# Output product of a hybrid decoder layer: seven half-size products in place of eight

## The chip, the cores and the metric

The kernel runs on one core of one Trainium2 chip. Its metric is the device time of one execution in microseconds (us), taken in three runs. TensorE (PE) multiplies matrices from SBUF into the eight banks of PSUM, VectorE (DVE) and ScalarE (ACT) read PSUM and SBUF, GpSimd (POOL) works from SBUF to SBUF, and SyncE (SP) issues DMAs.

## The reference, cut to what matters

```python
merged = sigmoid(g_a) * (y_a @ w_branch_a) + sigmoid(g_b) * (y_b @ w_branch_b)
x = x + gate[:, None, :] * (merged @ w_out)
```

`y_a` comes from a pooling branch, `y_b` from a sparse attention with top-k keys. All matrices are float32; `merged` is 1024 tokens by 1024 channels, `w_out` 1024 by 1024. This case is about the last line and the sum before it.

## The kernel before, in words

Every exact product is made of three passes: each operand is split into a high part (a copy rounded to the type fp32r) and a low part (what is left), and `product` (L727) adds high x high, high x low and low x high into one PSUM bank (L729 to L731). ACT makes the high parts, POOL or DVE the low ones by a subtraction.

The last part of the program goes as follows; times are of the profiled execution.

- Branch b (until 724): 16 units, each one bank of 128 channels by 512 tokens from 12 matmuls (`branch_b`, L1119). For each, DVE multiplies the bank by the stored sigmoid and adds branch a's share, read back from DRAM (`merge`, L2234, two tiles of `e_in`). This gives `m_raw`, the transposed `merged`, in four slots. ACT writes its high part `mT_hi`; the low part is made by POOL for even units (L1849) and by DVE for odd ones (`merge_low`, L2245). The order of units is the table `UNITS_B` (L158).
- The weights come in chunks of 256 columns and 1024 rows (four rows of 128 to a piece, `split_piece_hi` and `split_piece_lo`, L664 to L672), two chunks at a time. POOL splits w_branch_b's last two pieces and the first chunk of `w_out` beside the units; DVE splits the low parts of the other three (L1917, through `split_chunk_v`).
- Output product (724 to 813): `WO_ORDER` (L147) gives 20 units: 12 of 128 tokens by 512 columns (24 matmuls of 512) and 8 of 256 columns (24 of 256). Two banks alternate. DVE multiplies each by `gate` (L2304) and adds the rows of x (L2307), ACT issues the store (L1629), and SP loads the next rows.

Each engine runs its own list in order, with waits on semaphores; nothing reorders it. The order is written out by hand, and pools of PSUM banks are named by the table `pp_uses` with `pp_bank`: a use waits until the bank's previous use has been read.

Three smaller places are touched: the wait before the `ga` units (L1077), POOL's last `causal_scores` (L1719), and ACT's first use of SiLU in the attention part.

## Time and profile before

| | us |
|---|---|
| median of 3 runs (lowest to highest) | 816.81 (814.96 to 818.93) |
| profiled execution, its own time | 818.22 |
| its span, first to last instruction | 816.5 |
| busy: PE, DVE, ACT, POOL | 799.7, 579.0, 351.9, 336.7 |

The span is what the trace shows; the execution's own time is 1.7 us more. A matmul's row shows a duration that overlaps with the next one's, so the pace of PE is read from start to start. Starts of DVE instructions overlap their predecessors by less than 0.1 us. The mean granted clock of PE was 0.993 of full speed.

### The profile page before, as it was taken

To read this page: it belongs to the slowest core of one execution; us is meant where nothing else is said; L and a number is where in the kernel's file an instruction comes from. 1 tells how busy PE (TensorE), PEld (TensorE's weight loads), DVE (VectorE), ACT (ScalarE), POOL (GpSimd) and SP (SyncE) were. 2 spreads that over 40 slices of the span, in tenths; PEclk is the share of its full clock that TensorE was granted. 3 is DMA by queue.
4 is the path that set the end of the run, shared out by engine and by line. 5 is a ranking of instruction groups with operands and counts; after the bars stand their busy time and mean duration, and the time that the engine had idled before them with its cause. 6 is when DMAs were issued, how large, how long until landed. Compare 5 with 4: busy or idle time off the path is not lost.

```text
span 816.5 us, 12769 instructions
## 1 busy us (share of the span) xinstructions
PE 799.7 (98%) x4419; PEld 680.0 (83%) x4419; DVE 579.0 (71%) x1198; ACT 351.9 (43%) x644; POOL 336.7 (41%) x311
## 2 busy tenths in 40 slices
PE   7999999999999999999999999999999999999998
PEld 5988998887888888888878877789888897888987
DVE  5877478797888888898898716456667885772522
ACT  5665456664222212223241222687778883420100
POOL 1100524153445468852662212575888812540000
PEclk9899999999999999999999999999999999999999
DMA  9940110013242220331123323743433113753431
GB/s 342 386 126 1 53 52 27 1 41 121 103 123 78 91 90 16 102 96 46 52 78 103 104 78 107 236 138 114 130 105 115 40 40 137 252 168 123 131 101 58
DMA packets 59880, 87.87 MB, mean 108 GB/s; under 512 B 5513, under 2 KB 36525, under 8 KB 59822
## 3 DMA queue, kind: packets, MB, share of 16 engines
...
## 4 chain that ended last, share of the span: by engine, by line
PE 86%; DVE 6%; ACT 3%; issue 2%; DMA 1%; DVEq 1%; SPq 0%; POOLq 0%; POOL 0%; ACTq 0%
PE pp L729 21%; PE pp L730 21%; PE pp L731 21%; PE pp L1182 4%; PE pt L1157 3%; PE ps L970 3%; PE ps L969 3%; DVE score L2110 2%; DMA scale_w<-in_w_ada 1%; DVE prob L2268 1%; PE pt L1090 1%; DVE pT L2198 1%; PE ps L1067 1%; DVE ada_acc L1911 1%; PE pp L875 1%
## 5 line engine op out<-in xcount | busy, mean ns | idle before, releaser
L2135 DVE TENSOR_SCALAR_CACHE_REDUCE junk<-score,cand 128x384 uint8<-128x384 f32 (+1 forms) x186 | 168.6, 944 | 19.3 <-issue 13.3
L729 PE MATMUL pp<-hT_hi,w_hi 128*128 128x512 f32 x384 | 150.0, 390 | 0.8 <-ACT mixed L1511 0.8
L731 PE MATMUL pp<-hT_hi,w_lo 128*128 128x512 f32 x384 | 149.5, 389 | 0.0
L730 PE MATMUL pp<-hT_lo,w_hi 128*128 128x512 f32 x384 | 149.4, 389 | 0.0
L672 POOL TENSOR_TENSOR w_lo<-w_raw,w_hi 128x1024 fp32r<-128x1024 f32 x39 | 96.2, 2484 | 117.0 <-ACT w_hi L667 115.7
L729 PEld LDWEIGHTS pp<-hT_hi,w_hi 128*128 128x128 f32 x384 | 72.1, 188 | 16.1 <-ACT mixed L1511 1.3
L731 PEld LDWEIGHTS pp<-hT_hi,w_lo 128*128 128x128 f32 x384 | 72.1, 188 | 15.2
L730 PEld LDWEIGHTS pp<-hT_lo,w_hi 128*128 128x128 f32 x384 | 72.1, 188 | 14.7
L2198 DVE TENSOR_TENSOR pT<-pt,pT 128x512 fp32r<-128x512 f32 (+3 forms) x96 | 50.6, 555 | 45.0 <-ACT pT L1585 42.0
L1469 ACT ACTIVATE stage<-pp 128x512 f32<-128x512 f32 x32 | 19.2, 599 | 127.3 <-PE pp L731 127.3
L667 ACT ACTIVATE w_hi<-w_raw 128x1024 fp32r<-128x1024 f32 x52 | 52.8, 1054 | 44.8 <-PE pp L731 40.9
L729 PE MATMUL pp<-w_hi,hT_hi 128*128 128x256 f32 (+1 forms) x208 | 69.0, 332 | 1.8 <-POOL w_lo L672 1.1
L730 PE MATMUL pp<-w_lo,hT_hi 128*128 128x256 f32 (+1 forms) x208 | 67.5, 324 | 0.0
L731 PE MATMUL pp<-w_hi,hT_lo 128*128 128x256 f32 (+1 forms) x208 | 67.4, 324 | 0.0
L729 PE MATMUL pp<-w_hi,mT_hi 128*128 128x512 f32 (+1 forms) x160 | 55.6, 348 | 0.2 <-DVE o_row L2304 0.2
L730 PE MATMUL pp<-w_lo,mT_hi 128*128 128x512 f32 (+1 forms) x160 | 55.5, 347 | 0.0
L731 PE MATMUL pp<-w_hi,mT_lo 128*128 128x512 f32 (+1 forms) x160 | 55.5, 347 | 0.0
L729 PE MATMUL pp<-yT_hi,w_hi 128*128 128x512 f32 x128 | 52.7, 411 | 0.8 <-ACT a_out L1533 0.8
L1593 ACT ACTIVATE prob<-prob,neg_max 128x128 f32<-128x128 f32 (+7 forms) x64 | 49.8, 779 | 3.3 <-DVE neg_max L2268 3.0
L2110 DVE SCALAR_TENSOR_TENSOR score<-rel,w_idx,score 128x384 f32<-128x384 f32 (+5 forms) x42 | 43.7, 1042 | 9.3 <-ACT rel L1430 6.1
L2304 DVE TENSOR_TENSOR o_row<-pp,gate 128x512 f32<-128x512 f32 (+1 forms) x20 | 11.7, 584 | 54.3 <-PE pp L731 54.3
L730 PE MATMUL pp<-yT_lo,w_hi 128*128 128x512 f32 x128 | 50.1, 391 | 0.0
(311 smaller groups left out, 1834.2 us busy)
## 6 DMA issues: line engine op xcount, KB each, us to landing
w_raw<-in_w_in SPq DMA_DIRECT2D x36, 512.0 KB, 3.7
sgb_spill<-stage ACTq DMA_DIRECT2D x16, 256.0 KB, 2.0
sga_spill<-stage ACTq DMA_DIRECT2D x16, 256.0 KB, 2.0
stage<-sga_spill SPq DMA_DIRECT2D x16, 256.0 KB, 3.4
ma_spill<-stage POOLq DMA_DIRECT2D x16, 256.0 KB, 2.8
gate_w<-in_w_ada SPq DMA_DIRECT2D x16, 256.0 KB, 2.7
w_raw<-in_w_out SPq DMA_DIRECT2D x8, 512.0 KB, 4.7
e_in<-sgb_spill SPq DMA_DIRECT2D x16, 256.0 KB, 3.0
```

What stands on the lines that cost most here:

```text
L667: nc.scalar.activation(hi, raw, ACT.Copy).then_inc(w_hi_done, 1)
L672: nc.gpsimd.tensor_tensor(lo, raw, hi.bitcast(F32), ALU.subtract).then_inc(w_lo_done, 1)
L729: nc.tensor.matmul(o, a_hi, b_hi, start=first, stop=False)
L730: nc.tensor.matmul(o, a_hi, b_lo, start=False, stop=False)
L731: return nc.tensor.matmul(o, a_lo, b_hi, start=False, stop=last)
L969: nc.tensor.matmul(o[:, a:z], q, kt_[:, 0, a:z], start=True, stop=False)
L970: last = nc.tensor.matmul(o[:, a:z], q, kt_[:, 1, a:z], start=False, stop=True)
L1182: last = nc.tensor.matmul(pp[0][:, 0:2 * P], v2[:, t, :], pT[:, u % 2, t, s, :, :].rearrange("p h q -> p (h q)"), start=(t == 0 and s == 0 ...
L1593: nc.scalar.activation(prob[j % 4][:, 0:keys(b)], prob[j % 4][:, 0:keys(b)], ACT.Exp, scale=-1.0, bias=neg_max[:, j % 4:j % 4 + 1], accum_ ...
L2110: ins = v.scalar_tensor_tensor(s, rel[:, n % 2, 0:keys(b)], w, s, ALU.mult, ALU.add)
L2135: v.tensor_scalar(junk[:, n % 2, 0:keys(b)], score[:, score_at(b):score_at(b + 1)], least, None, ALU.is_ge, ALU.add, accum_out=cnt[:, n:n ...
L2198: v.tensor_tensor(pT[:, j // 2 % 2, t0:t1, 1, j % 2, :], pt[n % 2][:, 0:(t1 - t0) * P].rearrange("p (t q) -> p t q", q=P), pT[:, j // 2 % ...
```

## The change

The output product C = A W, with A the merged tokens by channels and W `w_out`, is cut into halves in tokens, channels and columns. Each quarter A11, A12, A21, A22 is 512 by 512, and so is each quarter of W. Seven products of quarters or of sums of them give C, where eight were made before:

S3 = A11 - A21, S1 = A21 + A22, S2 = S1 - A11, S4 = A12 - S2. The products, in order: A11 W11; S3 (W22 - W12); S2 (W22 - W12 + W11); A22 (W22 - W12 + W11 - W21); A12 W21; S1 (W12 - W11); S4 W22.

- `UNITS_B` is put in another order, so that units 0 to 3 are A11, 4 to 7 A21, and then A22 and A12 by turns of two. DVE makes S3, S1, S2, S4 from the merged units (`part_sums`) and the sums of the weights (`wo_sums`), with 16 loads of a piece of 512 KB instead of 8.
- High parts are ACT's. Low parts: POOL makes A11, A22, S1, A12 and the weights of products 1, 4, 5, 6, 7; DVE makes S3, S2, S4 and the weights of products 2 and 3.
- From unit 4 of branch b on, PSUM banks go in turn over six (the two of `ps` count as four halves).
- ACT copies the first two products into SBUF (`u1`, `u3`), DVE adds the others there (`u2`, `u3`), and rows of 512 columns are then multiplied by the gate and x is added, for four of the 16 by POOL.
- The wait before the `ga` units moves to the first tie transpose, one `causal_scores` moves behind a weight split, and a SiLU on one column is added to ACT ahead of a bank copy.

```diff
     UNITS_B = [(i, m, f) for f in range(2) for i in range(2) for m in range(2)]
-    UNITS_B += [(i, m, f) for i in range(2, 4) for f in range(2) for m in range(2)]
+    UNITS_B += [(i, m, f) for i in range(2, 4) for f in (1, 0) for m in range(2)]
+
+    M_PART = {(0, 0): "A11", (0, 1): "A21", (1, 0): "A12", (1, 1): "A22"}
+    UNIT_AT = {(M_PART[i // 2, f], 2 * (i % 2) + m): n for n, (i, m, f) in enumerate(UNITS_B)}
+    PART_OF = {n: part for part, n in UNIT_AT.items()}
...
+    PRODUCTS = ["A11", "S3", "S2", "A22", "A12", "S1", "S4"]
+    UPPER = [1, 0, 1, 0, 1, 0, 1]
+    STAGE_RAW = [0, 2, 2, 2, 0, 2, 0]
+    STAGE_BY_V = (1, 2)
+    W_LOADS = [(0, 0, 0), (0, 0, 1), (1, 1, 2), (1, 1, 3), (0, 1, 0), (0, 1, 1), (0, 0, 0), (0, 0, 1),
+               (1, 0, 0), (1, 0, 1), (0, 1, 2), (0, 1, 3), (0, 0, 0), (0, 0, 1), (1, 1, 0), (1, 1, 1)]
...
+    SUM_LOADS = [(2, 4), (6,), (8,), (10, 12)]
+    STAGE_SUM = {1: 0, 2: 1, 3: 2, 5: 3}
+    ROWS = 4
+    ROWS_BY_P = range(2 * ROWS, 3 * ROWS)
...
-    pp_bank += [(n + 1) % 2 for n in range(len(pp_uses) - len(pp_bank))]
+    pp_uses += [("wo", i, t) for i in range(len(PRODUCTS)) for t in range(4)]
+    pp_bank += [(n + 1) % 2 if n < 4 else [4, 5, 6, 7, 1, 0][(n - 4) % 6] for n in range(len(pp_uses) - len(pp_bank))]
...
+        pp += [ps[n // 2][:, n % 2 * HALF:(n % 2 + 1) * HALF] for n in range(4)]
...
+        WO_SLOT = [w_raw[:, (len(pieces) + n) % RAW] for n in (0, 1, 2)]
+        WO_RAW = [WO_SLOT[0], w_last[:], WO_SLOT[1], WO_SLOT[2]]
...
+                if u == min(MASK_UNIT):
+                    wait_done(pe, pp_done[pp_at[("mix", 1, 3)]], pp_free_a, pp_free_v)
...
-            wait_done(pe, pp_done[pp_at[("mix", 1, 3)]], pp_free_a, pp_free_v)
...
                     pe.wait_ge(w_lo_done, pieces_through[ci])
+                if k == 0 and n == 4:
+                    wait_done(pe, ps_done[-1], ps_free_a, ps_free_v)
+                    wait_done(pe, ps_done[-2], ps_free_a, ps_free_v)
...
+            for i, name in enumerate(PRODUCTS):
+                a_hi, a_lo = parts[name]
+                pe.wait_ge(wo_hi, 2 * i + 2)
+                wo_lo_wait(pe, i)
+                if name in ("S2", "S3", "S4"):
+                    part = (name, 3 if name == "S3" else 1)
+                    pe.wait_ge(part_lo_v, lo_v_at[part])
+                else:
+                    part = (name, 3)
+                    pe.wait_ge(part_lo_p, lo_p_at[part])
+                pe.wait_ge(part_hi, hi_at[part])
+                for t in range(4):
+                    o = pp_claim(("wo", i, t))
+                    tok = slice(t * P, (t + 1) * P)
+                    for k in range(4):
+                        kw = 4 * UPPER[i] + k
+                        last = product(o[:], a_hi[:, k, tok], a_lo[:, k, tok], w_hi[:, :, kw, :], w_lo[:, :, kw, :],
+                                       k == 0, k == 3)
+                    last.then_inc(pp_full, 1)
...
+                    if n == NSEL * H - 1:
+                        nc.scalar.activation(ssx[:, 0:1], ssx[:, 0:1], ACT.Silu)
...
+            def wo_high(st):
+                for a in range(2):
+                    hi, _, raw = wo_home(st, a)
+                    if st in STAGE_SUM:
+                        act.wait_ge(wo_sum, 2 * STAGE_SUM[st] + a + 1)
+                    else:
+                        j = STAGE_LOAD[st] + a
+                        act.wait_ge(wo_in[W_LOADS[j][2]], w_loaded[j])
+                    nc.scalar.activation(hi, raw, ACT.Copy).then_inc(wo_hi, 1)
...
+                if name == "A21":
+                    act.wait_ge(s3_done, k + 1)
+                    part_high("S3", k, gate_acc[:, k % 2 * HALF:(k % 2 + 1) * HALF])
+                    if k == 3:
+                        act.wait_ge(pp_full, chunk_done(name_of[("ga", 3)]))
+                        wo_high(0)
+                    continue
...
+                part_high(name, k, raw_m(n))
+                if name == "A22":
+                    act.wait_ge(s1_done, k + 1)
+                    part_high("S1", k, raw_21[:, k, :])
...
+            wo_high(1)
+            act.wait_ge(s2_done, 4)
+            for p in range(2):
+                pair_high("S2", p, raw_11)
+            keep(0, u1)
+            wo_high(2)
+            keep(1, u3)
+            act.wait_ge(s4_done, 4)
+            for p in range(2):
+                pair_high("S4", p, raw_21)
+            wo_high(3)
+            product_done(act, 2)
+            wo_high(4)
+            for n in range(4):
+                store(n)
+            product_done(act, 3)
+            wo_high(5)
+            for n in range(4, 8):
+                store(n)
+            product_done(act, 4)
+            wo_high(6)
+            for n in range(8, 16):
+                store(n)
...
-            causal_scores(NT - 1)
             pool.wait_ge(w_lo_done, pieces_through[name_of[("zb", 1)]] - 1)
             split_piece_lo(pool, pieces_through[name_of[("zb", 1)]] - 1)
+            causal_scores(NT - 1)
...
+            def part_low(name, k, raw):
+                hi, lo = parts[name]
+                pool.wait_ge(part_hi, hi_at[name, k])
+                gp.tensor_tensor(lo[:, k, :], raw, hi[:, k, :].bitcast(F32), ALU.subtract).then_inc(part_lo_p, 1)
+
...
+                if name == "A21":
+                    if k == 3:
+                        wo_low(0)
+                    continue
+                part_low(name, k, raw_m(n))
+                if name == "A22":
+                    part_low("S1", k, raw_21[:, k, :])
+            wo_low(3)
+            wo_low(4)
+            wo_low(5)
+            wo_low(6)
+            for n in ROWS_BY_P:
+                pool.wait_ge(c22_done, n - ROWS_BY_P[0] + 1)
+                pool.wait_ge(x_row_in[n % 4], 16 * (n // 4 + 1))
+                gp.tensor_tensor(o_row[:, n % 4, :], o_row[:, n % 4, :], x_row[:, n % 4, :], ALU.add).then_inc(o_row_p, 1)
...
+                if n >= 11:
+                    dve.wait_ge(part_hi, hi_at[PART_OF[n - 3]])
+                    dve.wait_ge(part_lo_p, lo_p_at[PART_OF[n - 3]])
...
+                v.tensor_tensor(raw_m(n), pp[pp_bank[u]][:], e_in[:, 0, n % 4, :], ALU.mult).then_inc(pp_free_v, 1)
+                dve.drain()
+                v.tensor_tensor(raw_m(n), raw_m(n), e_in[:, 1, n % 4, :], ALU.add).then_inc(m_raw_done, 1)
...
+            def part_sums(n):
+
+                name, k = PART_OF[n]
+                if name == "A11":
+                    return
+                dve.drain()
+                if name == "A21":
+                    if k == 0:
+                        dve.wait_ge(pt_full, pt_at[("gate", 1)] + 1)
+                    v.tensor_tensor(gate_acc[:, k % 2 * HALF:(k % 2 + 1) * HALF], raw_11[:, k, :], raw_21[:, k, :],
+                                    ALU.subtract).then_inc(s3_done, 1)
+                    if k:
+                        s3_low(k - 1)
+                elif name == "A22":
+                    if k == 0:
+                        s3_low(3)
+                    v.tensor_tensor(raw_21[:, k, :], raw_21[:, k, :], raw_m(n), ALU.add).then_inc(s1_done, 1)
+                    dve.drain()
+                    dve.wait_ge(part_hi, hi_at["A11", k])
+                    dve.wait_ge(part_lo_p, lo_p_at["A11", k])
+                    v.tensor_tensor(raw_11[:, k, :], raw_21[:, k, :], raw_11[:, k, :], ALU.subtract).then_inc(s2_done, 1)
+                else:
+                    dve.wait_ge(part_hi, hi_at["S1", k])
+                    dve.wait_ge(part_lo_p, lo_p_at["S1", k])
+                    v.tensor_tensor(raw_21[:, k, :], raw_m(n), raw_11[:, k, :], ALU.subtract).then_inc(s4_done, 1)
...
+                v.tensor_tensor(WO_RAW[2 + a], WO_RAW[2 + a], WO_RAW[a], op).then_inc(wo_sum, 1)
...
             for n in range(len(MERGE_AFTER), 16):
                 merge(n)
-                if n % 2 == 0:
-                    merge_low(n - 1)
-            merge_low(15)
-            split_chunk_v(name_of[("wo", 1)])
-
-            for n, (i, t) in enumerate(WO_ORDER):
+                part_sums(n)
+                if n >= 14:
+                    wo_sums(0, n - 14, ALU.subtract)
+            dve.drain()
+            wo_low(1)
+            for p in range(2):
+                pair_low("S2", p, raw_11)
+            for a in range(2):
+                wo_sums(1, a, ALU.add)
+            dve.drain()
+            wo_low(2)
+            for a in range(2):
+                wo_sums(2, a, ALU.subtract)
+
...
+            def finish_row(n):
+                o, c0 = o_row[:, n % 4, :], HALF * (n // 8)
+                dve.drain()
+                mult = v.tensor_tensor(o, o, gate[:, c0:c0 + HALF], ALU.mult)
+                if n in ROWS_BY_P:
+                    mult.then_inc(c22_done, 1)
+                    return
+                dve.drain()
+                dve.wait_ge(x_row_in[n % 4], 16 * (n // 4 + 1))
+                v.tensor_tensor(o, o, x_row[:, n % 4, :], ALU.add).then_inc(o_row_done, 1)
+            for t in range(4):
+                dve.wait_ge(pp_free_a, pp_done[pp_at[("wo", 1, t)]][0])
+                o = bank(2, t)
+                v.tensor_tensor(u2[:, t, :], o, u1[:, t, :], ALU.add).then_inc(pp_free_v, 1)
+                dve.drain()
+                v.tensor_tensor(u3[:, t, :], u2[:, t, :], u3[:, t, :], ALU.add)
+            for p in range(2):
+                pair_low("S4", p, raw_21)
+            dve.wait_ge(pt_free_a, pt_done[pt_at[("gate", 1)]][0])
+            dve.drain()
+            for t in range(4):
+                o, row = bank(3, t), take_row(t)
+                v.tensor_tensor(row, u3[:, t, :], o, ALU.subtract).then_inc(pp_free_v, 1)
+                finish_row(t)
+            for a in range(2):
+                wo_sums(3, a, ALU.subtract)
+            for t in range(4):
+                o, row = bank(4, t), take_row(4 + t)
+                v.tensor_tensor(row, o, u1[:, t, :], ALU.add).then_inc(pp_free_v, 1)
+                finish_row(4 + t)
```

The first place where instructions move is DVE's row at branch b's unit 8, of before:

```order
L2242 TENSOR_TENSOR m_raw<-pp0,e_in 128x512
L2244 TENSOR_TENSOR m_raw<-m_raw,e_in 128x512
L2242 TENSOR_TENSOR m_raw<-pp1,e_in 128x512
L2244 TENSOR_TENSOR m_raw<-m_raw,e_in 128x512
L2249 TENSOR_TENSOR mT_lo<-m_raw,mT_hi 128x512
```

Two units take five instructions there. Now, units 8 and 9 (both of A22) and the first of A12 on the same engine, where raw_x is the merged unit, raw_11 and raw_21 hold A11 and A21 and then the sums:

```order
L2428 TENSOR_TENSOR raw_x<-pp1,e_in 128x512
L2430 TENSOR_TENSOR raw_x<-raw_x,e_in 128x512
L2435 TENSOR_TENSOR S3_lo<-gate_acc,S3_hi 128x512
L2454 TENSOR_TENSOR raw_21<-raw_21,raw_x 128x512
L2458 TENSOR_TENSOR raw_11<-raw_21,raw_11 128x512
L2428 TENSOR_TENSOR raw_x<-pp0,e_in 128x512
L2430 TENSOR_TENSOR raw_x<-raw_x,e_in 128x512
L2454 TENSOR_TENSOR raw_21<-raw_21,raw_x 128x512
L2458 TENSOR_TENSOR raw_11<-raw_21,raw_11 128x512
L2428 TENSOR_TENSOR raw_x<-ps0,e_in 128x512
L2430 TENSOR_TENSOR raw_x<-raw_x,e_in 128x512
L2462 TENSOR_TENSOR raw_21<-raw_x,raw_11 128x512
```

A unit of A22 has four instructions and one of A12 three; the low parts of A22, S1 and A12 went to POOL. POOL's last rows of before:

```order
L1849 TENSOR_TENSOR mT_lo<-m_raw,mT_hi 128x512 x3
L672 TENSOR_TENSOR w_lo<-w_raw,w_hi 128x1024
L1849 TENSOR_TENSOR mT_lo<-m_raw,mT_hi 128x512
L672 TENSOR_TENSOR w_lo<-w_raw,w_hi 128x1024
L1849 TENSOR_TENSOR mT_lo<-m_raw,mT_hi 128x512 x2
L672 TENSOR_TENSOR w_lo<-w_raw,w_hi 128x1024 x2
L1849 TENSOR_TENSOR mT_lo<-m_raw,mT_hi 128x512 x2
```

And now, from the same instant (the start of branch b's merges) to the middle of the A22 and A12 units:

```order
L2008 TENSOR_TENSOR A11_lo<-raw_11,A11_hi 128x512 x4
L779 TENSOR_TENSOR w_lo<-w_raw,w_hi 128x1024 x2
L2014 TENSOR_TENSOR w_lo<-w_raw,w_hi 128x1024
L2014 TENSOR_TENSOR w_lo<-w_last,w_hi 128x1024
L2008 TENSOR_TENSOR A22_lo<-raw_x,A22_hi 128x512
L2008 TENSOR_TENSOR S1_lo<-raw_21,S1_hi 128x512
L2008 TENSOR_TENSOR A22_lo<-raw_x,A22_hi 128x512
L2008 TENSOR_TENSOR S1_lo<-raw_21,S1_hi 128x512
L2008 TENSOR_TENSOR A12_lo<-raw_x,A12_hi 128x512 x2
```

Eight parts of 512 became sixteen (eight are shown up to the last row's two of A12, the other six follow in the same pattern), and the four of 1024 stay four, two of them now for the first product.

## Rows read from the trace of the kernel before

**Rows 1.** The page: busy us of each engine, share of span, instructions.
```profile
PE 799.7 (98%) x4419; PEld 680.0 (83%) x4419; DVE 579.0 (71%) x1198; ACT 351.9 (43%) x644; POOL 336.7 (41%) x311
```

**Rows 2.** Windows: length, busy of PE, PEld, DVE, ACT, POOL, clock, DMA, GB/s.
```profile
690.00:724.00 34.00, 34.00 (x151) 27.86 (x149) 27.69 (x34) 13.25 (x19) 21.28 (x11) 1.00 0.68 220
724.00:814.00 90.00, 89.01 (x481) 77.20 (x480) 32.62 (x50) 6.73 (x8) 1.29 (x1) 1.00 0.34 110
```

**Rows 3.** Timeline of VectorE in the output product; start us, us.
```profile
785.73 0.69 DVE L2304 TENSOR_TENSOR o_row<-pp,gate 128x512 f32<-128x512 f32 x1 [3.96 <-PE pp L731]
...
791.17 0.69 DVE L2304 TENSOR_TENSOR o_row<-pp,gate 128x512 f32<-128x512 f32 x1 [3.96 <-PE pp L731]
...
813.24 0.42 DVE L2304 TENSOR_TENSOR o_row<-pp,gate 128x256 f32<-128x256 f32 x1 [1.93 <-PE pp L731]
```

**Rows 4.** Timeline of TensorE, first output units of 256 columns.
```profile
724.39 0.28 PE L730 MATMUL pp<-w_lo,mT_hi 128*128 128x256 f32 x1
...
729.67 0.28 PE L729 MATMUL pp<-w_hi,mT_hi 128*128 128x256 f32 x1
```

**Rows 5.** Tile m_raw and line L672: ns min/median/max, first and last start.
```profile
L2242 DVE TENSOR_TENSOR m_raw<-pp,e_in x16: 677/692/693, 683.2 to 724.2; 128x512 f32<-128x512 f32 x16
L2244 DVE TENSOR_TENSOR m_raw<-m_raw,e_in x16: 692/892/1169, 684.0 to 725.0; 128x512 f32<-128x512 f32 x16
...
L1849 POOL TENSOR_TENSOR mT_lo<-m_raw,mT_hi x8: 1293/1306/1747, 691.0 to 724.2; 128x512 fp32r<-128x512 f32 x8
L2249 DVE TENSOR_TENSOR mT_lo<-m_raw,mT_hi x8: 678/685/2883, 691.4 to 726.8; 128x512 fp32r<-128x512 f32 x8
...
L672 POOL TENSOR_TENSOR w_lo<-w_raw,w_hi x39: 2381/2407/3165, 101.8 to 717.0; 128x1024 fp32r<-128x1024 f32 x39
```

**Rows 6.** Timeline of VectorE from 711 to 728.
```profile
711.38 0.69 DVE L2244 TENSOR_TENSOR m_raw<-m_raw,e_in 128x512 f32<-128x512 f32 x1
711.99 0.69 DVE L2249 TENSOR_TENSOR mT_lo<-m_raw,mT_hi 128x512 fp32r<-128x512 f32 x1
...
716.82 0.79 DVE L2244 TENSOR_TENSOR m_raw<-m_raw,e_in 128x512 f32<-128x512 f32 x1
717.53 2.88 DVE L2249 TENSOR_TENSOR mT_lo<-m_raw,mT_hi 128x512 fp32r<-128x512 f32 x1
720.34 0.68 DVE L2242 TENSOR_TENSOR m_raw<-pp,e_in 128x512 f32<-128x512 f32 x1
721.11 1.01 DVE L2244 TENSOR_TENSOR m_raw<-m_raw,e_in 128x512 f32<-128x512 f32 x1
...
727.40 2.48 DVE L1917 TENSOR_TENSOR w_lo<-w_raw,w_hi 128x1024 fp32r<-128x1024 f32 x2
```

**Rows 7.** Timeline of GpSimd from 714 to 722.
```profile
714.46 5.41 POOL L672 TENSOR_TENSOR w_lo<-w_raw,w_hi 128x1024 fp32r<-128x1024 f32 x2 [0.35 <-ACT w_hi L667]
719.83 1.74 POOL L1849 TENSOR_TENSOR mT_lo<-m_raw,mT_hi 128x512 fp32r<-128x512 f32 x1
```

**Rows 8.** Waits of TensorE: total us, times, longest.
```profile
PE pp L729 <- ACT mixed L1511: 0.8, 1, 0.8
```

**Rows 9.** The page's DMA issues: KB each, median us to landing.
```profile
w_raw<-in_w_out SPq DMA_DIRECT2D x8, 512.0 KB, 4.7
...
out<-o_row ACTq DMA_DIRECT2D x12, 256.0 KB, 3.0
```

**Rows 10.** Last bisection step, first tie transpose, and a table load.
```profile
462.14 0.16 DVE L2151 TENSOR_TENSOR thr<-thr,accept 128x6 int32<-128x6 int32 x1
...
L1055 PE MATMUL pt<-ident_b,eq x33: 219/219/230, 476.3 to 510.9; 128*128 128x128 bf16 x33
...
188.16 1.28 ACT L1395 ACT_TABLE_LOAD   x1
```

**Rows 11.** TensorE's gaps from 185 to 195, in brackets.
```profile
189.89 0.38 PE L729 MATMUL pp<-w_hi,hT_hi 128*128 128x256 f32 x1 [0.45 <-ACT zb_out L1395]
...
194.12 0.50 PE L729 MATMUL pp<-w_hi,hT_hi 128*128 128x512 f32 x1 [1.09 <-POOL w_lo L672]
```

289 lines of the change are left out of this document (178 added, 111 removed).

## The prediction

> **What bounds the kernel now.** I read the page first, then the stretches, then single rows. TensorE (PE) is busy 98% of the span [rows 1]. The output product runs from 724.2 to 813.2, and in both stretches of the tail PE is busy without a break at a granted clock of 1.00 [rows 2]. One 512-column unit of 24 matmuls takes 791.17 - 785.73 = 5.44 us, so 0.227 us a matmul, and a 256-column one costs 0.12 (44 starts from 724.39 to 729.67) [rows 3, 4]. So work taken from PE there is worth its full price, if nothing else is late instead.
>
> What could be late is the second thing to see. While branch b is projected (690 to 724), VectorE (DVE) is busy 27.7 of 34 us and GpSimd (POOL) 21.3 [rows 2], and they are not independent. A DVE add or low part, with both inputs in SBUF, has a shortest time of 0.68 to 0.69 us, but 0.892 in the middle and 2.883 at the longest; the multiply of the same size that reads PSUM stays within 0.677 to 0.693 [rows 5]. The instants say why [rows 6, 7]. POOL's two weight splits last from 714.46 to 719.87. DVE's low part issued at 717.53, inside the second, ends at 720.41, which is 0.54 behind POOL's end. POOL's next, issued at 719.83, lasts 1.74 instead of 1.30 and ends at 721.57, 1.16 behind that DVE end. DVE's add, issued at 721.11, ends at 722.12, 0.55 behind that. They take turns, whole instructions at a time.
>
> A page of the Trainium skill has a rule for it. "SBUF — State Buffer", section "SBUF: two separate sides", says that DVE and GpSimd share a port pair which one instruction holds to its end, and that a DVE instruction takes it when both inputs are in SBUF. The trace agrees (2.883 against 0.68). If both engines ran at once, as their separate queues suggest, the sum below would end near rival A; by the rule it is the forecast. The steps themselves need only the rows.
>
> **The change: what PE gains.** Before, PE runs 12 x 24 matmuls at 0.227 and 8 x 24 at 0.12: 65.3 + 23.0 = 88.3 us. After, 7 products x 4 units x 12 = 336 matmuls of 512 columns: 76.2 us. It gains 12.1, and up to 0.7 of small gaps (813.2 less 724.2 less 88.3). Started at 724.2 and never late, PE would end at 800.4. Six banks in turn take away no wait of branch b, where PE is busy 34.00 of 34.00 us [rows 2].
>
> **What DVE and POOL get.** I count what needs the turn, from 691.0 (POOL's first low part) to where the second product, S3, can start. S3's weight parts come from DVE, and stand behind all merges, part sums and the first weight sum.
> - DVE, 512 wide: 14 adds (units 2 to 15), 4 S3 sums, 4 S3 low parts, 4 each of S1, S2, S4 = 34. Alone one takes 0.61 from start to start (711.38 to 711.99 [rows 6]): 20.7 us.
> - DVE, 1024 wide: two weight sums, two low parts, at 2.48 / 2 = 1.24 [rows 6]: 5.0 us.
> - POOL, 512 wide: 16 low parts (A11, A22, S1, A12), between 1.16 (waiting) and 1.30 (alone); 1.2: 19.2 us. Before there were 8.
> - POOL, 1024 wide: two pieces of w_branch_b and the two of the first product, between 2.26 (waiting: 719.87 less 717.61, the end of DVE's add) and 2.41 (alone) [rows 5 to 7]; 2.35: 9.4 us.
>
> Together 54.3 us, from 691.0 to 745.3. The same count for the kernel before (14 adds, 8 low parts, 8 and 4 on POOL) gives 32.4 of the 36.5 us to 727.5, the end of its last low part, so there it is nearly full already, though PE never waits. POOL's share can't be put off: from unit 11 DVE's multiply waits for the low part of the unit three before (three raw buffers), and each S4 sum for POOL's S1 low part. And the turn is idle where DVE multiplies, 0.77 us (720.34 to 721.11), and POOL has no backlog; writing the instructions down one by one with these durations I find about 3.2 us of it, mostly at units 5 to 7. S3 starts at 748.6. Without lateness it would start at 724.2 + 10.9 = 735.1. **PE waits 13.5 us here**; bounds 9.2 (735.1 to 744.3, no idle turn and the last A12 low part later) and 17 (0.69, 1.30 and 2.41 throughout: 34 x 0.08 + 16 x 0.1 more, less what fills idle turns).
>
> **Products 2 to 4** are ready: behind S3's start DVE needs two S2 low parts, two sums and two low parts (6 x 1.24 = 7.4) within 10.9. The loads, 4.7 us each [rows 9], are asked for as each sum ends. Nothing late.
>
> **S1, the sixth.** Its weight sum stands on DVE behind four rows of the fourth product, each two times 0.69 with some 0.1 of drain and once 0.69, 2.3 us (three operations where before there were two). By the same writing down S3 ends 759.5, S2 770.4, A22 781.2, A12 792.1. DVE first has S4's low parts, which take turns with POOL's splits for A12 to about 777.6, then the four rows (779 to 787.5), the sums to 789.7, then POOL two splits with DVE's work between: 794.9. **2.8 late**; bounds 0 and 4.5.
>
> **S4, the last.** ScalarE (ACT) issues the stores of rows 4 to 7 before it makes the last high part, and row 7 is done near 801.9. One high part of about 1 us later POOL's 2 x 2.4 with DVE between gives 809.1, where PE would be ready at 805.9. **3.2 late**; bounds 0 and 5.
>
> **The end.** Before, 3.3 us from the last matmul (813.2) to the end of the span, with two DVE operations of 0.42 in it [rows 3]. After, three operations of 512 columns (2.3), the store's issue and 3.0 to land [rows 9]: 5.8 us, at most 6.3. **2.5 to 3 more.**
>
> **The middle.** The wait for the last mix banks moves from the start of the ga units to unit 11; PE waited 0.8 for it [rows 8]. What follows is PE's until 476.3, when the tie transposes start, and DVE's bisection ended at 462.3 [rows 10], so it stays gained: -0.8 (bounds -1 and 0). The early SiLU table load (1.28 [rows 10]) now comes in front of a bank copy that PE needs, at 186, and takes away a wait of 0.45 at 189.9 [rows 11]; both run into the 1.09 us wait for POOL's split at 194.1, which follows a DVE split not moved. So 0 (bounds -0.5 and +1). causal_scores moving behind a split of 2.4 us [rows 5] has 13 us of slack before 476.3. 0.
>
> **Sum.** 724.2 + 76.2 + 13.5 + 2.8 + 3.2 = 819.9 for PE's end; + 5.8 = 825.7; - 0.8 = 824.9 for the span, 8.4 over 816.5. The profiled execution took 818.22 for its span of 816.5, the median of the runs is 816.81: 1.41 less. So 818.22 + 8.4 = 826.6 on its own scale, and 825.2 on the median's. I say 825.3.
>
> **Rivals.** (A) DVE and POOL do not get in each other's way in the new order: DVE then needs from 694.4 (unit 4's end) 12 multiplies of 0.77, 32 x 0.61, drains of some 0.15 and 5.0, so until about 731, in time for 735.1; S1 and S4 are in time too. 800.4 + 5.8 - 0.8 = 805.4, the median 805.7: 11 faster. For it speaks that PE never waited on the merges before; against it rows 5 to 7. (B) Turns are taken, but only S3 at its lower bound of 9.2 is late: 800.4 + 9.2 + 5.8 - 0.8 = 814.6, median 814.9, within 0.5% of before. For it speaks that S1 and S4 are each late by some 3 us only, at the end of a chain of DVE, ACT and POOL work of more than 20; against it, that the lower bound leaves the turn never idle. (C) The turn and the forecast's mechanism, with prices at their upper bounds, 17 + 4.5 + 5 and 6.3: 800.4 + 26.5 + 6.3 - 0.8 = 832.4, median 832.7, a slower case of the same sign. (D) Weight loads are late: 16 instead of 8 through four slots. At 4.7 us each and asked for more than 8 us ahead, save the second of W11 and of W21 (5 us ahead), it costs under 2.
>
> **Chances.** 0.70 for the forecast with C, 0.14 for B and what lies near it, 0.16 for A. The point from which it is slower: the gains 12.1, 0.7 and 0.8 less 2.5 at the end are 11.1 us, so the three latenesses together must pass 11.1; by S3 alone, where it starts behind 746. Within 0.5% (4.1 us) is about what a measurement of this kernel can't tell from no change. Faster by more 0.17, within 0.13, slower 0.70. The range is 813 to 832; A alone, and a little above, lies outside. The likeliest case's own range is 819 to 832.
>
> **What the profile will show.** If right: PE idle some 13 us behind A11's product, at about 736, released by DVE's weight low part; smaller gaps of about 3 us before the sixth and seventh products, released by POOL; DVE's two-SBUF-input adds stretched to a median above 1.1 us between 691 and 745, POOL over 75% busy there, multiplies still 0.69; PE matmuls 0.227 apart. Wrong if S3 starts by 738, if the adds stay at 0.7 to 0.9, or if a wait of PE falls on a bank or a load.

## The result

The changed kernel takes 827.88 us (median of 6 runs, 826.28 to 833.5), the kernel before 817.55 (814.82 to 819.21) on the same chips: ratio 1.0152, 95% interval 1.013 to 1.0174. That is slower by 12.4 us by the ratio (one of the waits below is as long by chance). The forecast was slower, at 825.3; the mechanism is the one forecast, with one term missing and three of another size.

The profiled execution took 827.83 us for a span of 826.1. Its page, and TensorE's waits from 690 on (line, what released it, total us, times, longest):

```profile
PE 790.4 (96%) x4275; PEld 667.2 (81%) x4275; DVE 636.5 (77%) x1236; ACT 368.8 (45%) x667; POOL 375.0 (45%) x331
```

```profile
PE pp L836 <- DVE w_lo L2474: 12.4, 1, 12.4
PE ps L836 <- issue: 4.5, 2, 3.2
PE ps L836 <- DVE raw_x L2428: 0.8, 1, 0.8
```

TensorE has 9 us less to do than in [rows 1] and stands for 17.7 us in places where it did not stand before. The stretches of the tail (columns as in [rows 2], which they answer):

```profile
690.00:724.00 34.00, 33.88 (x150) 27.75 (x149) 31.27 (x29) 9.92 (x14) 22.30 (x12) 1.00 0.50 158
724.00:745.00 21.00, 8.42 (x36) 6.30 (x34) 19.55 (x20) 7.33 (x11) 9.77 (x7) 0.83 0.37 121
745.00:830.00 85.00, 70.40 (x288) 57.02 (x288) 65.48 (x69) 17.35 (x22) 26.82 (x12) 0.91 0.46 152
```

PE works 8.4 of the 21 us from 724 while DVE is busy for 19.6, and the granted clock, 1.00 throughout in [rows 2], is 0.83 and 0.91.

**A ruler.** The first stage varies from execution to execution, also where two kernels are the same there: the selection's last wait on ScalarE ends between 178.1 and 182.2 in the 14 profiles taken. So I compare two stretches that don't contain it. The *middle* goes from the end of that wait to the last transposes of the branch stage, the *tail* from there to the end of the span. The four instants, of before and of after:

```profile
181.29 0.50 PE L969 MATMUL ps<-kiT,qiT 128*128 128x512 f32 x1 [0.68 <-ACT rel L1430]
...
688.12 0.60 PE L758 MATMUL pt<-ident,y_row 128*128 128x128 f32 x4
```

```profile
178.13 0.50 PE L1076 MATMUL ps<-kiT,qiT 128*128 128x512 f32 x1 [0.68 <-ACT rel L1540]
...
684.83 0.60 PE L865 MATMUL pt<-ident,y_row 128*128 128x128 f32 x4
```

Before: 506.8 and 816.5 - 688.12 = 128.4. After: 506.7 and 826.1 - 684.83 = **141.3, 12.9 more**. Instants of the tail after stand 3.29 earlier than the same ones on before's scale. Kernels that do the same in the tail differ there by no more than 0.2 us (before and e9_mix_alone 128.4 each, after 141.3 and e7_no_silu 141.5), so a tail, though it comes from one profile, tells smaller differences than the ratios do.

**The turns.** (A turn is the time of one instruction with two SBUF operands, during which such an instruction of the other engine doesn't get on.) GpSimd and VectorE at the A22 units and in the output stage (start us, us):

```profile
708.14 2.55 POOL L2014 TENSOR_TENSOR w_lo<-w_raw,w_hi 128x1024 fp32r<-128x1024 f32 x1 [2.24 <-ACT w_hi L1739]
710.65 2.85 POOL L2014 TENSOR_TENSOR w_lo<-w_last,w_hi 128x1024 fp32r<-128x1024 f32 x1
...
718.20 1.30 POOL L2008 TENSOR_TENSOR A_lo<-raw_x,A_hi 128x512 fp32r<-128x512 f32 x1 [1.30 <-ACT A_hi L1725]
719.46 1.74 POOL L2008 TENSOR_TENSOR S_lo<-raw,S_hi 128x512 fp32r<-128x512 f32 x1
```

```profile
708.53 2.71 DVE L2435 TENSOR_TENSOR S_lo<-gate_acc,S_hi 128x512 fp32r<-128x512 f32 x1
711.16 2.88 DVE L2454 TENSOR_TENSOR raw<-raw,raw_x 128x512 f32<-128x512 f32 x1
...
718.40 1.65 DVE L2458 TENSOR_TENSOR raw<-raw 128x512 f32<-128x512 f32 x1 [0.16 <-issue]
719.97 0.68 DVE L2428 TENSOR_TENSOR raw_x<-ps,e_in 128x512 f32<-128x512 f32 x1
720.74 1.01 DVE L2430 TENSOR_TENSOR raw_x<-raw_x,e_in 128x512 f32<-128x512 f32 x1
```

Each of the first two DVE rows ends 0.54 to 0.55 behind the POOL row it was issued in (711.24 behind 710.69, 714.04 behind 713.50). The fourth, of 719.97, reads PSUM and keeps its 0.68 beside a running POOL instruction.

**The clock.** PE behind its long wait, and the windows around it:

```profile
745.56 0.77 PE L836 MATMUL pp<-w_hi,S_hi 128*128 128x512 f32 x1 [12.38 <-DVE w_lo L2474]
746.13 0.63 PE L837 MATMUL pp<-w_lo,S_hi 128*128 128x512 f32 x1
746.55 0.63 PE L838 MATMUL pp<-w_hi,S_lo 128*128 128x512 f32 x1
...
751.58 0.40 PE L838 MATMUL pp<-w_hi,S_lo 128*128 128x512 f32 x1
751.81 0.39 PE L836 MATMUL pp<-w_hi,S_hi 128*128 128x512 f32 x1
...
795.31 0.47 PE L836 MATMUL ps<-w_hi,S_hi 128*128 128x512 f32 x1 [3.21 <-issue]
...
809.33 0.47 PE L836 MATMUL ps<-w_hi,S_hi 128*128 128x512 f32 x1 [1.29 <-issue]
```

```profile
747.00:749.00 2.00, 2.00 (x6) 1.61 (x5) 2.00 (x3) 1.04 (x3) 0.00 (x0) 0.50 0.00 0
...
752.00:757.00 5.00, 5.00 (x23) 4.13 (x22) 2.91 (x3) 0.83 (x2) 0.00 (x0) 1.00 0.90 305
```

The granted clock is 0.50, the lower level, behind the wait, and matmuls start 0.42 to 0.43 apart (746.13, 746.55) until 751.3, then 0.23. The products from S3 to A12 take 795.31 - 3.21 - 745.56 = 46.5 us, against 4 x 10.9 = 43.6: 2.9 for the clock. S1, behind its 3.2 us wait, takes 809.33 - 1.29 - 795.31 = 12.7 for 10.9: 1.8.

### The profile page after: what moved, and what is told of

Read it like the earlier page. It is cut to its first block, busy times and chain, and to the rows that moved or that the text cites. A ratio compares the mean times of both kernels' runs of the same rounds, so it can differ in the third digit from the quotient of the medians.

```text
span 826.1 us, 12619 instructions
## 1 busy us (share of the span) xinstructions
PE 790.4 (96%) x4275; PEld 667.2 (81%) x4275; DVE 636.5 (77%) x1236; ACT 368.8 (45%) x667; POOL 375.0 (45%) x331
## 4 chain that ended last, share of the span: by engine, by line
PE 77%; DVE 10%; DVEq 6%; issue 3%; ACT 3%; POOL 1%; DMA 0%; POOLq 0%; ACTq 0%
PE pp L836 17%; PE pp L838 17%; PE pp L837 16%; PE pp L1294 3%; PE pt L1269 3%; PE ps L1077 3%; PE ps L1076 3%; DVEq L2429 3%; DVE score L2293 2%; DVEq L2540 1%; DVE o_row L2541 1%; DVE raw_x L2430 1%; PE pp L872 1%; PE pt L895 1%; PE ps L837 1%
## 5 line engine op out<-in xcount | busy, mean ns | idle before, releaser
L779 POOL TENSOR_TENSOR w_lo<-w_raw,w_hi 128x1024 fp32r<-128x1024 f32 x37 | 90.4, 2460 | 129.9 <-ACT w_hi L774 121.0
L2492 DVE CUSTOM_DVE_ANT_0 prob<-ps,bias 128x128 f32<-128x128 f32 (+7 forms) x64 | 47.9, 748 | 3.0 <-PE ps L1077 1.5
L1697 ACT ACTIVATE pT<-pt 128x512 fp32r<-128x512 f32 (+3 forms) x96 | 43.9, 492 | 11.9 <-PE pt L1269 10.9
L774 ACT ACTIVATE w_hi<-w_raw 128x1024 fp32r<-128x1024 f32 x44 | 44.7, 1052 | 4.0 <-ACT stage L1581 2.7
L1269 PE MATMUL pt<-ident,prob 128*128 128x128 f32 x288 | 44.4, 277 | 1.8 <-ACT qT L1664 1.1
L1540 ACT ACTIVATE rel<-ps 128x384 f32<-128x384 f32 (+5 forms) x48 | 36.3, 759 | 19.2 <-PE ps L1077 11.2
L836 PEld LDWEIGHTS pp<-w_hi,hT_hi 128*128 128x128 f32 x208 | 40.2, 193 | 4.2 <-ACT q_all L1477 2.0
L838 PEld LDWEIGHTS pp<-w_hi,hT_lo 128*128 128x128 f32 x208 | 40.2, 193 | 3.3
```

Source lines behind the costliest of these rows:

```text
L774: nc.scalar.activation(hi, raw, ACT.Copy).then_inc(w_hi_done, 1)
L779: nc.gpsimd.tensor_tensor(lo, raw, hi.bitcast(F32), ALU.subtract).then_inc(w_lo_done, 1)
L836: nc.tensor.matmul(o, a_hi, b_hi, start=first, stop=False)
L838: return nc.tensor.matmul(o, a_lo, b_hi, start=False, stop=last)
L1269: last = nc.tensor.transpose(o[:, (t % 4) * P:(t % 4 + 1) * P], prob[j % 4][:, t * P:(t + 1) * P], ident[:])
L1697: nc.scalar.activation(pT[:, j // 2 % 2, t0:t1, 0, j % 2, :], o[:, 0:(t1 - t0) * P].rearrange("p (t q) -> p t q", q=P), ACT.Copy).then_inc ...
```

## The experiments

Theory T: DVE and POOL take turns wherever both read two SBUF operands, and the added sums and low parts make that queue longer than TensorE's work; behind its waits TensorE then also runs at the lower clock. Rival R1: DVE's own list is too long, whatever POOL does. Rival R2: a load, or a chain of dependent steps, is late. A *part* is below a quarter of A or a sum of two (low parts of 512 columns), a *split* the low part of a weight piece (1024 columns), and a *fill* writes zeros and reads nothing. What each kernel took (ratios against the kernel before, run on the same chips):

| kernel | median us | ratio, 95% interval | tail us |
|---|---|---|---|
| before | 816.0 to 817.6 | 1 | 128.4 |
| after | 827.88 | 1.0152 (1.013 to 1.0174) | 141.3 |
| e1_fill | 819.59 | 1.0043 (1.0028 to 1.0059) | 132.3 |
| e2_twice | 830.97 | 1.0170 (1.0147 to 1.0194) | 143.3 |
| e3_s1_vector | 831.05 | 1.0172 (1.015 to 1.0193) | 141.7 |
| e4_early | 822.84 | 1.0065 (1.0044 to 1.0085) | 134.9 |
| e5_warm | 826.73 | 1.0122 (1.0103 to 1.014) | 139.4 |
| e6_late | 828.75 | 1.0153 (1.0122 to 1.0183) | 140.4 |
| e7_no_silu | 828.76 | 1.0158 (1.0134 to 1.0181) | 141.5 |
| e8_best | 822.58 | 1.0080 (1.0057 to 1.0103) | 134.7 |
| e9_mix_alone | 815.18 | 0.9987 (0.9972 to 1.0001) | 128.4 |
| e10_fill_all | 806.69 | 0.9867 (0.9841 to 0.9894) | 118.1 |
| e11_fill_early | 806.04 | 0.9854 (0.9827 to 0.9882) | 117.0 |
| e12_weights_on_vector | 816.84 | 1.0004 (0.9989 to 1.0019) | 129.5 |

**Take POOL's turns away: e1_fill, e10_fill_all.**

```diff
-                gp.tensor_tensor(lo[:, k, :], raw, hi[:, k, :].bitcast(F32), ALU.subtract).then_inc(part_lo_p, 1)
+                gp.memset(lo[:, k, :].bitcast(F32), 0.0).then_inc(part_lo_p, 1)
```

> The changed kernel, with GpSimd's low parts of A11, A22, S1 and A12 (16 subtractions that read two SBUF operands, 1.2 us each in the tally) written as fills with zeros, which read nothing; the low parts of these are left out of the product. Waits, order and signals stay. Theory T (VectorE and GpSimd take turns, a whole instruction each, where both read two SBUF operands): the 19.2 us of these subtractions leave the sequence in which VectorE stands, so the wait of 12.4 us before S3's product falls to 0 to 2 us, the matmuls behind it stay 0.227 us apart instead of 0.427 (2.8 us), VectorE's eight additions to raw_x fall from a mean of 0.93 us towards 0.61 to 0.7, and the kernel comes to about 813 us (809 to 818), about 15 us less than the changed kernel. Rival R1 (VectorE's own list of work up to S3 is too long, whatever GpSimd does): wait and durations as they were, 827 to 828. Rival R2 (a load or the activations' products come late): the same, 827 to 828, with the wait put down to a transfer or to ScalarE.

The tail is 9.0 us shorter. The merged units' additions and multiplies of after, then of this kernel (ns min/median/max):

```profile
L2430 DVE TENSOR_TENSOR raw_x<-raw_x,e_in x8: 693/996/1042, 707.7 to 739.2; 128x512 f32<-128x512 f32 x8
...
L2428 DVE TENSOR_TENSOR raw_x<-ps,e_in x4: 675/680/685, 720.0 to 729.4; 128x512 f32<-128x512 f32 x4
```

```profile
L2430 DVE TENSOR_TENSOR raw_x<-raw_x,e_in x8: 691/692/693, 706.8 to 731.6; 128x512 f32<-128x512 f32 x8
...
736.80 0.76 PE L836 MATMUL pp<-w_hi,S_hi 128*128 128x512 f32 x1 [5.10 <-issue]
```

No edit touched DVE, and its additions fell from 996 to 692 ns; the multiply from PSUM had nothing to lose. The size was missed: I expected the wait to be 0 to 2 us and it is 5.1, and the kernel takes 819.6 and not some 813. Of the 12.4 us, 7.3 are POOL's turns for parts; the next run divides the 5.1.

e10 does the same to POOL's ten splits of output weights (`gp.tensor_tensor(lo, raw, ...)` in `wo_low` becomes `gp.memset(lo, 0)`), and leaves those low parts out too.

> e1_fill with GpSimd's low parts of the output weights (10 subtractions of 1024 columns) written as zero fills too; those low parts are left out. Theory T: VectorE's stretched instructions in the output stage (2.89, 2.11, 2.88, 4.55 for two, 2.35, 2.67, 1.52, 1.48, 1.66 us in the profile after) fall to 0.69 (2.35 for the two of 1024 columns), the low parts are ready 3 us sooner, and the waits before S1's and S4's products (4.5 us together) and their half clock (1 us) go: e1's 819.6 less 5.5 less up to 1 at the end, 813 us (811 to 815.5). Rival (those waits come from loads and from where the sums stand in VectorE's list, as e6 hints for S4): 816 to 819, and the stretched instructions shrink without moving the end.

```profile
PE pp L836 <- issue: 0.9, 1, 0.9
```

One wait of 0.9 us is left in the whole tail, and VectorE's sixteen multiplies by the gate have a mean of 695 ns. It won 6 us more than expected, because the first product's two splits (708 to 713) are fills too, and most of the 5.1 us that e1 had left before S3 was theirs, with the lower clock behind it. What R1 has of the 12.4 us is at most the 0.9. The tail of 118.1 is 10.3 less than before; rival A of the prediction, no turns at all, was 12.1 + 0.7 - 2.5 = 10.3 less, and 805.7 us, where 806.7 was measured. So the seven products do save what they should. GpSimd's low parts of the output product cost 141.3 - 118.1 = 23.2 us of tail. That isn't turns alone, since fills are also shorter than subtractions (0.53 and 0.95 us against 1.3 and 2.4), so what waits for them starts sooner. Before S3's product VectorE's rows settle it: the parts and the first product's two splits stretch its instructions by 13.5 us there, and 11.5 of the wait went with them. How much of the rest is length, no run separates.

**Double four of them: e2_twice.**

```diff
+                if name == "S1":
+                    gp.tensor_tensor(lo[:, k, :], raw, hi[:, k, :].bitcast(F32), ALU.subtract)
+                    pool.drain()
                 gp.tensor_tensor(lo[:, k, :], raw, hi[:, k, :].bitcast(F32), ALU.subtract).then_inc(part_lo_p, 1)
```

> The changed kernel, with each of GpSimd's four low parts of S1 computed twice in a row (the same values written again). GpSimd was busy for 9.8 of the 21 us before S3's product, so in its own list there is room for four more subtractions. Theory T: each costs a turn of 1.2 us in VectorE's list as well, so the wait before S3's product grows from 12.4 to about 17 us and the kernel to about 832.5 us (830 to 835). Rival R1 (VectorE's own list is the bound) and R2 (late data): no change, 827 to 828.5, since GpSimd has the room.

The wait grew from 12.4 to 14.0 and the tail by 2.0 us. R1 and R2 said no change; T said 4.8 us, more than twice too much. **Move four of them: e3_s1_vector** puts the same four on VectorE (`v.tensor_tensor(lo[:, j, :], raw_21[:, j, :], ...)` in the next unit, with its wait on their high part).

> The changed kernel, with the four low parts of S1 computed on VectorE instead of GpSimd. VectorE has more to do by four subtractions, GpSimd less. Theory T: a subtraction costs VectorE's sequence 1.2 us when GpSimd does it and 0.61 us when VectorE does it, so the wait before S3's product falls by 2.4 us and the kernel to about 825.5 us (824 to 827). Rival R1 (only VectorE's own list counts): the wait grows by 4 x 0.61 = 2.4 us, 830.3 us. These are opposite signs for the same edit.

The tail is 141.7 against 141.3, the wait 12.5. T expected 2.4 us less and R1 2.4 more, and neither came. (The ratio of 1.0172 would allow R1; the tail doesn't.) The rows of one A22 unit tell why. After: 715.68 to 719.97, 4.29 us a unit. Here:

```profile
718.49 0.68 DVE L2426 TENSOR_TENSOR raw_x<-pp,e_in 128x512 f32<-128x512 f32 x1
719.26 0.69 DVE L2428 TENSOR_TENSOR raw_x<-raw_x,e_in 128x512 f32<-128x512 f32 x1
719.87 0.68 DVE L2445 TENSOR_TENSOR S_lo<-raw,S_hi 128x512 fp32r<-128x512 f32 x1
720.64 0.69 DVE L2458 TENSOR_TENSOR raw<-raw,raw_x 128x512 f32<-128x512 f32 x1
721.50 1.54 DVE L2462 TENSOR_TENSOR raw<-raw 128x512 f32<-128x512 f32 x1 [0.16 <-issue]
722.96 0.68 DVE L2426 TENSOR_TENSOR raw_x<-ps,e_in 128x512 f32<-128x512 f32 x1
```

4.47. VectorE took 0.6 us more, and POOL's turn that went had cost it only some 0.4, not 1.2: it used to run beside the multiply from PSUM (719.46 to 721.20 beside 719.97 to 720.65), where VectorE doesn't need the turn. **A POOL instruction costs the other engine its length less what of it lies beside work that needs no turn.** VectorE's rows of after, each against its length alone (0.69 us, 1.22 for 1024 columns), say the same: POOL's 16 parts stretch them by 9.3 us, 0.6 each and not the 1.2 that these three runs were forecast with; the first product's two splits by 4.2, 2.1 each, and w_branch_b's two by 4.2. As a count of how long the turn is taken, the prediction's tally still holds: from POOL's first low part (687.67) to the end of S3's weight low parts (745.5) it is held or waited for during 53.1 us and idle for 4.7, against 54.3 and 3.2. It just isn't a price: when POOL's turn goes, VectorE's multiplies, which ran beside it, are still to be done.

**Keep TensorE busy while it waits: e5_warm.**

```diff
+                if name in ("S3", "S1"):
+                    keep_warm(50 if name == "S3" else 12, pp_claim(("wo", i, 0))[:])
                 pe.wait_ge(wo_hi, 2 * i + 2)
```

> The changed kernel, with TensorE kept busy while it waits: 50 matmuls of 512 columns on constants, whose result is overwritten, before S3's product, and 12 before S1's. The waits themselves stay. If the granted clock falls because TensorE stood idle (theory C, the term that the prediction lacked), S3's matmuls come 0.227 us apart from its first one instead of 0.427 for the first 5.7 us, which is 2.8 us, and S1's the same for 4 us, which is 2.0 us: 823 us (822 to 825). If the lower clock has another cause (load on the chip, or the change of the kind of work), the spacing stays 0.427 and the kernel stays at 827 to 829.

```profile
735.15 10.96 PE L872 MATMUL pp<-prefix,ident_b 128*128 128x512 bf16 x50 [1.23 <-DVE raw_x L2430]
746.30 0.47 PE L836 MATMUL pp<-w_hi,S_hi 128*128 128x512 f32 x1 [0.18 <-issue]
746.61 0.39 PE L837 MATMUL pp<-w_lo,S_hi 128*128 128x512 f32 x1
746.84 0.40 PE L838 MATMUL pp<-w_hi,S_lo 128*128 128x512 f32 x1
```

S3's matmuls are 0.23 apart at once and the granted clock is 1.00 from 745 to 795: the lower clock comes from standing still. But the tail is 1.9 us shorter, not 4.8. The wait before S4 grew from 1.29 to 2.85, and S4 had the lower clock in turn (0.86 from 800 to 812): the output stage's VectorE and GpSimd are as late as before, and PE waits for them later. A clock term ahead of another wait wasn't worth its length here.

**Other orders of the same work: e4_early, e6_late, e7_no_silu, e8_best.** e4 takes the first weight sum, high and low part into the part stage (ScalarE's high part and two loads move along; VectorE's lines are shown):

```diff
-                if n >= 14:
-                    wo_sums(0, n - 14, ALU.subtract)
-            dve.drain()
-            wo_low(1)
+                if n == 11:
+                    for a in range(2):
+                        wo_sums(0, a, ALU.subtract)
+                if n == 12:
+                    wo_low(1)
```

> The changed kernel, with the output weights' first sum, its high part and its low part (wo_sums(0), wo_high(1), wo_low(1)) not behind the whole part stage but in it: VectorE does the sum after unit 11 and the low part after unit 12, ScalarE the high part after unit 11. The amount of work is the same. Theory T says that the first wait is a matter of how much two-operand work stands in turn ahead of S3: moving the weights' work ahead by itself leaves the same total, but it takes away the chain sum, high, low, in which VectorE waits, at the end. Expected: the wait of 12.4 us falls by 5 to 7, the kernel to about 821 us (819 to 824). If the total of turns alone sets the time (T in its strict form): within 1 us of the changed kernel, 827 to 829. If the wait is only a matter of the chain at the end (R3: placement, not amount): the wait nearly goes, 814 to 817.

```profile
PE ps L835 <- DVE raw_x L2428: 5.5, 2, 2.9
```

6.4 us less tail, as expected: PE now waits twice for a merged unit (2.6 and 2.9) and not for S3. So placement is worth half of the loss as long as the turns are there; without them it is worth 1.1 us (e11 below). e6 does the like with the last sums and, on ScalarE, the last high parts, which go ahead of stores (VectorE's lines are shown):

```diff
                 finish_row(t)
-            for a in range(2):
-                wo_sums(3, a, ALU.subtract)
+                if t == 1:
+                    for a in range(2):
+                        wo_sums(3, a, ALU.subtract)
```

> The changed kernel, with the last sums of output weights (wo_sums(3)) made after the second output row instead of behind all of S3's, and with ScalarE's high parts 5 and 6 taken ahead of the stores' turn. The same work in another order. Theory D (the 3.2 us wait before S1's product and the 1.3 us before S4's are the chain sum, high part, low part of the weights, which starts late because of where it stands in each engine's list): both waits go, and with the first of them the 4 us at half clock (2.0 us): 823 us (821 to 825). Theory T alone (GpSimd's low parts of 5.2 us for two are what is late, because they take turns with VectorE's output work): they start earlier but take as long, so half of it or less is won, 825 to 827.

0.9 less tail, where some 5 us were expected, and no difference in the times. S1's wait went, S4's grew from 1.3 to 3.6, because the last weights were now awaited:

```profile
802.82 1.06 ACT L1739 ACTIVATE w_hi<-w_raw 128x1024 fp32r<-128x1024 f32 x1 [13.15 <-DMA w_raw<-in_w_out]
...
809.51 0.77 PE L836 MATMUL ps<-w_hi,S_hi 128*128 128x512 f32 x1 [3.65 <-issue]
```

```profile
784.17 12.75 SPq L672 DMA_DIRECT2D x_row<-in_x  x4
796.97 0.43 SPq L678 DMA_DIRECT2D w_raw<-in_w_out  x1
```

The sum that frees the buffer ended at 787.4, but the load stands in SyncE's queue behind four row loads, each of which waits until VectorE has used the row before; it was issued at 796.97 and landed 5.8 us later. R2 is right there, as soon as the other cause is taken away; e8, which has this edit too, shows the same (its last weights' high part starts at 794.36, behind the load).

e7 leaves out the early SiLU activation (`nc.scalar.activation(ssx[:, 0:1], ssx[:, 0:1], ACT.Silu)`).

> The changed kernel without the one SiLU activation that was put behind the last score of the selection, ahead of the table's use. In the trace after, TensorE's wait on q_all grew from 0.2 to 1.75 us where this activation stands, and the start of the next stage moved by 0.9 us against the start of the selection. If that is the activation: the wait shrinks to what it was, 0.9 us less, 827.0 us (826.3 to 827.7), and a table load is then seen in the next stage's ScalarE rows. If the load just moves and is waited for there: no change.

No gain. My 0.9 came from one profile. The early load does raise the wait on q_all from 0.24 to 1.75 us, and takes away 0.46 and 0.8 behind it. The middle is 505.6 to 505.7 in eleven of the thirteen profiles with the moved mix wait, with the load and without; in two with the load (after, e10) it is 506.6 to 506.7, with a granted clock of 0.91 from 180 to 200, right behind that wait. So the load is worth 0. Whether it is also what brings the 1 us of clock isn't shown (two of nine profiles with it, none of four without). e8 joins the three edits.

> The changed kernel with the edits of e4_early, e6_late and e7_no_silu together. Added up: 827.9 less 6.3 (measured, from the first of the merged units to the end) less 5.2 (e6's expectation) less 0.9 gives 815.5 us (813 to 819), against 816.7 before: a Strassen stage that costs nothing, and perhaps a little better. If the turns bound the end as well, the later waits only move and it stays at 819 to 822.

Its tail is e4's, and its 822.58 us are 7 more than expected. In both, DVE works through the output stage nearly without a break, stretched by POOL's eight splits (in e8 by 14.9 us).

**Move the splits: e12_weights_on_vector.** This is e8 with POOL's eight splits of the fourth to seventh product on VectorE:

```diff
-    STAGE_BY_V = (1, 2)
+    STAGE_BY_V = (1, 2, 3, 4, 5, 6)
...
                 v.tensor_tensor(u3[:, t, :], u2[:, t, :], u3[:, t, :], ALU.add)
+                if t == 1:
+                    wo_low(3)
             for p in range(2):
                 pair_low("S4", p, raw_21)
+            wo_low(4)
```

and `wo_low(5)`, `wo_low(6)` on VectorE behind the rows of the fourth and fifth product.

> e8_best with the low parts of the output weights for the 4th to 7th product (8 subtractions of 1024 columns) moved from GpSimd to VectorE: 9.1 us of work more in VectorE's list (8 x 1.14). In e8_best the eight cost GpSimd 21.8 us and stretch VectorE's instructions beside them: 2.12, 2.11, 6.76 for a pair, 2.36, 2.73, 2.62, 2.67 us against 0.69 (2.35 for the pair), 14.2 us in all. Theory T as the runs have left it (a whole instruction of the other engine is waited for; VectorE's own subtraction is half as long as GpSimd's): VectorE's time from 757 us to the end falls by 14.2 - 9.1 = 5 us, of which 2 to 4 reach the end, 819.5 us (818 to 821), 3 less than e8_best's 822.6. Rival R1 (VectorE's own list is what counts): 9.1 us more in an output stage in which VectorE is busy throughout, 826 to 831. As in e3_s1_vector, where the turn was hidden beside a multiplication from PSUM, the gain can come out as nothing: 822 to 823.

VectorE behind the S2 product in e8, and here:

```profile
763.68 0.68 DVE L2552 TENSOR_TENSOR u<-pp,u 128x512 f32<-128x512 f32 x1
...
767.16 6.76 DVE L2479 TENSOR_TENSOR S_lo<-raw,S_hi 128x1024 fp32r<-128x1024 f32 x2
774.01 0.69 DVE L2561 TENSOR_TENSOR o_row<-u,ps 128x512 f32<-128x512 f32 x1
```

```profile
762.80 0.68 DVE L2548 TENSOR_TENSOR u<-pp,u 128x512 f32<-128x512 f32 x1
...
765.97 2.35 DVE L2475 TENSOR_TENSOR S_lo<-raw,S_hi 128x1024 fp32r<-128x1024 f32 x2
768.24 1.22 DVE L2470 TENSOR_TENSOR w_lo<-w_raw,w_hi 128x1024 fp32r<-128x1024 f32 x1
769.37 1.22 DVE L2470 TENSOR_TENSOR w_lo<-w_last,w_hi 128x1024 fp32r<-128x1024 f32 x1
```

**The busier engine got 9 us more work and the kernel became 5.7 us faster** (822.58 to 816.84, and by the ratios 6.2; tail 5.2), 2.7 more than expected. R1 would have it slower. The 14.9 us of stretch less the 9.1 of work are 5.8. The edit changes two things at once, though: the turns go, and a pair of low parts takes 2.35 us where POOL took 5.2 or more. For the wait of 2.5 us before S4, of which nothing is left, no run parts the two. What is left are the waits of 2.6 and 4.3 us for merged units, as in e8, with a granted clock of 0.64 in the 6 us behind the second:

```profile
PE ps L835 <- DVE raw_x L2424: 6.8, 2, 4.3
```

This is the seven-product kernel at the time of the one before, ratio 1.0004 (0.9989 to 1.0019).

**What helps alone: e9_mix_alone** is the kernel before with the moved wait:

```diff
-            wait_done(pe, pp_done[pp_at[("mix", 1, 3)]], pp_free_a, pp_free_v)
...
+                if u == min(MASK_UNIT):
+                    wait_done(pe, pp_done[pp_at[("mix", 1, 3)]], pp_free_a, pp_free_v)
                 if u in MASK_UNIT:
                     tie_transposes(MASK_UNIT[u])
```

> The kernel before, with one thing of the change alone: TensorE's wait for the last mixed unit stands ahead of the first tied block's transposes instead of behind all of the selection's. In ten profiles the stretch from the selection's last wait to the last transposes of the branch stage is 506.8 us before and 505.7 with the change (506.7 in the one profile after, which had 1 us at half clock in it). Expected: 1.2 us less than before, ratio 0.9985, so about 815.3 us where before is 816.5. If the gain comes from elsewhere in the change (banks, the order of units), the ratio is 1.000.

Its middle is 505.7 against 506.8, as forecast; the ratio's interval just touches 1. It is the fastest of the kernels that leave nothing out: 815.18 us.

**The ceiling: e11_fill_early** is e10 with e4's edit.

> e10_fill_all with the edit of e4_early (the output weights' first sum, high and low part inside the part stage). With no turns left, what remained in e1 was a wait of 5.1 us before S3's product for VectorE's own list, and about 4 us at half clock behind it (2 us). If that is placement, both go and the kernel comes to 806.5 us (804 to 809), the seven products' whole saving of 12 us less the longer end. If VectorE's own list is full, part of it stays: 809 to 813.

No wait of PE in the tail. It is 1.1 us less than e10 (117.0), because e10 had only 0.9 left to win; the gain of the placement depends on the turns. Most of what I expected of it had already gone in e10.

## Why the prediction was right, and where it was off

- **S3's wait, the main step.** S3 starts at 745.56 + 3.29 = 748.85 on before's scale; forecast 748.6. PE's waits up to there are 12.4 + 0.8 = 13.2, forecast 13.5. e1 and e10 show the cause. Its tally of turns held too (57.8 us from POOL's first low part to S3, forecast 57.6). What failed is to read 1.2 us a subtraction out of it as a price, as the expectations of e1 to e3 did: e2 and e3 show 0.5 and 0.4.
- **The signs in the profile were in part misplaced.** The additions' median is 1.0 and not above 1.1; the stretch sits on a few (groups of after, busy us, mean ns), up to 2.89, and POOL is busy 32 of 55 us, 58%, not 75. The multiplies stay at 0.68, as said.

```profile
L2430 DVE TENSOR_TENSOR raw_x<-raw_x,e_in 128x512 f32<-128x512 f32 x8 | 7.4, 930 | 0.7
L2435 DVE TENSOR_TENSOR S_lo<-gate_acc,S_hi 128x512 fp32r<-128x512 f32 x4 | 7.0, 1739 | 0.1
L2458 DVE TENSOR_TENSOR raw<-raw 128x512 f32<-128x512 f32 x4 | 6.5, 1621 | 0.6 <-issue 0.6
```

- **Products 2 to 4, the loads.** No wait; right.
- **S1.** 3.2 late (forecast 2.8). **S4.** 1.3 (3.2): the wait mis-sized most. POOL's last low part ends 3.4 us later than forecast, but TensorE is ready 5.4 later, mostly through the clock. The small wait is no success of the sum, it hides 2 us of the missing term.
- **The clock: a term that the sum lacked.** The sum puts nothing for the clock, and its sign "PE matmuls 0.227 apart" failed: 2.9 + 1.8 us at the lower clock. e5 shows that the cause is standing still, and that only 1.9 of the 4.7 reach the end.
- **The end.** PE ends at 820.5 (its last matmul is issued at 820.09), the span at 826.1: 5.6 (forecast 5.8).
- **The middle.** -1.1 to -1.2 for the moved wait (forecast -0.8; a little outside its bound of -1); SiLU 0, right, with 1 us of clock in two profiles.
- **The sum.** Forecast for the tail: 819.9 + 5.8 - 816.5 = 9.2. Measured 12.9; the 3.7 between are 4.7 of clock, 0.4 of S1, less 1.9 of S4, 0.3 of S3's wait and 0.2 of the end, and some 1.0 of small gaps: 0.55 ahead of S3's product (it starts 0.25 later than forecast behind waits that are 0.3 shorter), some 0.3 in S4's product and its last row, and rounding. So the time of 825.3 was near for a sum that lacked 4.7 us and had 1.9 too much elsewhere; that part is luck.
- **Rivals.** A's price (10.3 us of tail) is what e10 measured, and its condition false. Its list for VectorE, until about 731, agrees: in e10 the list ends at 735.8 on before's scale with 4.2 us of w_branch_b's turns still in it. That the tails agree to the tenth is luck, since e10 has these turns and shorter fills. B fell with the 12.4 us. C's prices were too high. D is nothing here; a load is late for S4 in e6 and e8 only.
